# mLSTM and neighbourhood attention on one core: weights' low parts one item later, the first scores ahead of the last transposes, the closing norm's steps one item later on two engines

## The chip, the cores and the metric

The kernel runs on one core of a Trainium2 chip. The metric is the device time of one execution in microseconds (us): the median of three runs, beside which one more execution was profiled. A core has one instruction queue for each of its engines: TensorE (PE in the rows; PEld is its weight load), VectorE (DVE), ScalarE (ACT), GpSimd (POOL) and SyncE (SP, which here only issues DMAs). The queues run side by side and meet at semaphores: an instruction waits until a semaphore has reached a number, and raises one when it is done.

## What is computed

Two stacks of two layers follow one another on 256 tokens of width 1024. The change lies in the even mixer of the second stack, in two of its parts.

```python
def even_mixer(hx, hc, ...):              # hx: 256 latent tokens, hc: 256 context tokens
    naq, nak, nav, mlqk, mlv, mlo, mlg = split(h @ w_in)
    na_x = neighbourhood_attention(...)   # 8 heads of 64, latent queries: window + all context keys
    h_xf, h_xb = mlstm_chunked(...)       # 4 heads of 128, forward and backward, chunks of 128
    ml_x = _mlstm_output(h_xf + _rev(h_xb), mlo_x, ml_norm_g)
    y_x = concatenate([na_x, ml_x]) @ w_out
    na_c = dense_attention(...)           # context queries, context keys
    ...                                   # y_c likewise

def _mlstm_output(h, o_pre, g):           # the gate, then the closing norm over each head
    h = sigmoid(o_pre) * h
    mu = mean(h); var = mean(square(h - mu))
    return (h - mu) * rsqrt(var + EPS) * g
```

## The kernel before

All is float32; 512 tokens (256 context, 256 latent) lie in four tiles of 128. Products with large weights are split: of a weight tile RAW the high part WHI is a cast (ACT, `high`, L1516), the low part WLO = RAW - WHI a subtraction (DVE, `rest`, L2170), and TensorE adds three products of such halves. A unit is 1 MB of weights; `split(n)` makes TensorE wait for its low part, and SP loads a unit once the work on the unit that had its slot is done.

Each engine's program is written out by hand, so the order below is the order of the code. There are no pools and no scheduler.

**The mLSTM stage** has 16 items n, head h = n // 4 and query tile t = n % 4. For each, DVE makes the exponents' arguments (`args`, L2696 to L2701), ACT the exponentials (L1948, L1949), TensorE the scores (`score`), DVE weighs and normalises them (`weigh`, L2712 to L2723, result PR), TensorE transposes them (`turn(n)`, L1161), ACT copies the transposed tile out (`copy_turned`, L1927), and TensorE multiplies it with the values (`values(n)`). TensorE does `turn(n)` and then `values(n - 1)`. Between `score(n + 1)` and `turn(n)` it does six parts of the attention's input projections (`na_part`), which fill its time; ACT takes each finished tile of these out (`na_take`, L1934 and L1937). Six weight units, EVEN0 + 10 to EVEN0 + 15, are split in this stage, in the items ML_UNITS_AT = (1, 4, 6, 9, 12, 14): `high` is ACT's last work of such an item, `rest` DVE's. The first four of them are for `na_part`, the last two for the output projection. Once a head is complete, DVE multiplies it by the output gate (`gate(h)`, L2728, which waits for the head's last values).

**The attention stage** has 16 pairs p of heads (`EVEN_PAIRS`): eight with 256 keys, then eight with 512 keys and a bias. For pair p DVE finds two row maxima (`top(p)`, L2765, L2766), ACT makes the exponentials (`weights(p)`, L1986), DVE normalises them (`norm(p)`, L2773, L2775), TensorE transposes (`turn(p)`, L1245), ACT copies (L1996), TensorE multiplies with the values, ACT casts the high part of the result (`place_high`, L2002) and DVE subtracts for the low part (`place`, L2781). Orders by pair: TensorE `scores(p + 2), turn(p), values(p - 1)`; DVE `top(p + 1), norm(p), place(p - 2)`; ACT `weights(p + 1)`, copies of p, `place_high(p - 1)`. PR and PRE are two pairs of buffers, taken in turn.

**The closing norm** of the mLSTM (`head_norm`) is spread over the attention's pairs: after its own work each engine calls it with n = 2p - 2 and 2p - 1. For the four heads there is a mean product on TensorE (at n in MEAN_AT = 0, 3, 6, 9), a centring on DVE (L2747), a square on ACT (L1966); one variance product at n = 13; logarithm and exponential at 14 and 15 (ACT); then a product that spreads the inverse root (SPREAD_AT = 16, 19, 22, 25; weight operand HSTD), a scaling on DVE (L2751), a cast on ACT (L1976) and a subtraction on DVE (L2756). Every product of the norm goes to PSUM bank 7 and waits until DVE or ACT has read the one before.

After the last pair, the output projection waits for all 16 `place` and the four subtractions of the norm.

## Time and profile before

| | us |
|---|---|
| median of three runs | 2146.18 (2145.66 to 2146.91) |
| the profiled execution | 2143.44 |
| its span, first to last instruction | 2141.6 |
| PE busy in the span | 2097.8 |
| DVE busy in the span | 1525.0 |
| ACT busy in the span | 1060.0 |
| mLSTM stage in the span | about 1171 to 1281.5 |
| attention stage in the span | about 1281.5 to 1353.6 |

A row of the timeline gives the start of an instruction, or of several alike that follow one another, counted from the span's start, its time, the engine, the line, what is written and read, the count, and in brackets how long the engine was idle just before and who ended that. Durations of matmuls are modelled, and each overlaps the next; the distance between two starts says how long one occupies the engine. On DVE and ACT too a following instruction can start some 0.1 us before the row of the last one ends.

### The profile page before, as it was taken

To read this page: it belongs to the slowest core of one execution; us is meant where nothing else is said; L and a number is where in the kernel's file an instruction comes from. 1 tells how busy PE (TensorE), PEld (TensorE's weight loads), DVE (VectorE), ACT (ScalarE), POOL (GpSimd) and SP (SyncE) were. 2 spreads that over 40 slices of the span, in tenths; PEclk is the share of its full clock that TensorE was granted. 3 is DMA by queue.
4 is the path that set the end of the run, shared out by engine and by line. 5 is a ranking of instruction groups with operands and counts; after the bars stand their busy time and mean duration, and the time that the engine had idled before them with its cause. 6 is when DMAs were issued, how large, how long until landed. Compare 5 with 4: busy or idle time off the path is not lost.

```text
span 2141.6 us, 35228 instructions
## 1 busy us (share of the span) xinstructions
PE 2097.8 (98%) x14796; PEld 1922.4 (90%) x14796; DVE 1525.0 (71%) x2351; ACT 1060.0 (49%) x1578; POOL 156.1 (7%) x195
## 2 busy tenths in 40 slices
PE   9999999999999999999999998999999999999997
PEld 8999989999999998999997774898888888589997
DVE  7878888878988798998852666456555335857774
ACT  6443656443644465644462446345444334746663
POOL 1200102200210100210100000000000001000000
PEclk9999999999999999999999999999999999999999
DMA  7665526667566543777431120113222222123552
GB/s 286 231 238 203 209 99 249 243 228 273 193 241 230 206 177 118 282 269 264 149 111 66 60 68 38 49 58 132 99 99 99 99 79 95 43 79 122 190 182 99
DMA packets 48334, 334.93 MB, mean 156 GB/s; under 512 B 5612, under 2 KB 6716, under 8 KB 8880
## 3 DMA queue, kind: packets, MB, share of 16 engines
q1 hardware_dynamic: 38384, 267.47, 35.3%
q0 software_dynamic: 9792, 65.21, 8.1%
q8 instruction: 117, 1.92, 0.4%
q14 instruction: 41, 0.34, 0.0%
HBM read 331.61 MB, written 1.05 MB: 155 GB/s over the span
## 4 chain that ended last, share of the span: by engine, by line
PE 90%; DVE 5%; ACT 2%; issue 1%; DMA 0%; POOL 0%; DVEq 0%; ACTq 0%; POOLq 0%
PE PS L475 88%; PE PS L1245 1%; DVE WLO L2170 1%; ACT WHI L1516 1%; DVE STAT L2765 0%; DMA RAW<-in_up_a 0%; DVE TM L2712 0%; DVE AC L2613 0%; PE PS L1161 0%; DVE ACC L2410 0%; DVE TM L2696 0%; DVE PT L2454 0%; ACT X L1548 0%; DVE XB L2255 0%; DVE X L2597 0%
## 5 line engine op out<-in xcount | busy, mean ns | idle before, releaser
L2170 DVE TENSOR_TENSOR WLO<-RAW,WHI 128x2048 fp32r<-128x2048 f32 (+1 forms) x251 | 573.2, 2288 | 212.3 <-ACT WHI L1516 209.7
L475 PE MATMUL PS<-XB,WHI 128*128 128x256 f32 (+1 forms) x3136 | 703.6, 320 | 7.9 <-DVE WLO L2170 4.4
L1516 ACT CAST WHI<-RAW 128x2048 fp32r<-128x2048 f32 (+1 forms) x247 | 467.2, 1894 | 271.0 <-DMA RAW<-in_dn_c 75.4
L475 PEld LDWEIGHTS PS<-XB,WHI 128*128 128x128 f32 x3136 | 523.4, 191 | 52.9 <-issue 5.1
L475 PE MATMUL PS<-XHI,WHI 128*128 128x272 f32 (+1 forms) x1760 | 498.5, 290 | 0.1
L475 PE MATMUL PS<-XB,WLO 128*128 128x256 f32 (+1 forms) x1568 | 498.3, 318 | 0.0
L475 PE MATMUL PS<-XHI,WLO 128*128 128x272 f32 (+1 forms) x1760 | 489.4, 287 | 0.0
L475 PE MATMUL PS<-XLO,WHI 128*128 128x272 f32 (+1 forms) x1760 | 481.2, 287 | 0.0
L475 PEld LDWEIGHTS PS<-XHI,WHI 128*128 128x128 f32 x1760 | 328.4, 188 | 1.7 <-issue 0.7
L475 PEld LDWEIGHTS PS<-XHI,WLO 128*128 128x128 f32 x1760 | 325.7, 188 | 0.2
L475 PEld LDWEIGHTS PS<-XLO,WHI 128*128 128x128 f32 x1760 | 322.2, 188 | 1.4 <-DVE XLO L2216 0.8
L475 PEld LDWEIGHTS PS<-XB,WLO 128*128 128x128 f32 x1568 | 299.6, 191 | 20.1
L475 PE MATMUL PS<-GHI,WHI 128*128 128x272 f32 (+1 forms) x704 | 200.3, 286 | 0.0
L475 PE MATMUL PS<-GHI,WLO 128*128 128x272 f32 (+1 forms) x704 | 199.7, 285 | 0.0
L2613 DVE SCALAR_TENSOR_TENSOR AC<-CB,FCW,AC 128x512 f32<-128x512 f32 (+1 forms) x176 | 97.1, 614 | 133.7 <-ACT AC L1835 105.1
L475 PE MATMUL PS<-GLO,WHI 128*128 128x272 f32 (+1 forms) x672 | 191.9, 286 | 0.0
L475 PEld LDWEIGHTS PS<-GHI,WLO 128*128 128x128 f32 x704 | 132.5, 188 | 0.0
L475 PEld LDWEIGHTS PS<-GHI,WHI 128*128 128x128 f32 x704 | 132.4, 188 | 0.0
L2199 DVE CUSTOM_DVE_ANT_0 PROD<-AW,SCB,ADAB 128x1024 f32<-128x1024 f32 x96 | 131.4, 1368 | 0.0
L1623 ACT ACTIVATE SG<-PS 128x272 f32<-128x272 f32 (+1 forms) x88 | 34.5, 393 | 195.2 <-PE PS L475 194.8
L2199 DVE CUSTOM_DVE_ANT_0 AW<-AW,SCB,ADAB 128x1024 f32<-128x1024 f32 x96 | 127.1, 1324 | 0.0
L475 PEld LDWEIGHTS PS<-GLO,WHI 128*128 128x128 f32 x672 | 126.4, 188 | 0.0
(372 smaller groups left out, 2464.9 us busy)
## 6 DMA issues: line engine op xcount, KB each, us to landing
AW<-in_ada POOLq DMA_DIRECT2D x48, 1024.0 KB, 7.2
RAW<-in_up_c SPq DMA_DIRECT2D x44, 1024.0 KB, 4.9
RAW<-in_up_a SPq DMA_DIRECT2D x42, 1024.0 KB, 5.2
RAW<-in_up_b SPq DMA_DIRECT2D x42, 1024.0 KB, 5.0
RAW<-in_mix SPq DMA_DIRECT2D x30, 1024.0 KB, 4.9
RAW<-in_dn_a SPq DMA_DIRECT2D x22, 1024.0 KB, 4.9
RAW<-in_dn_b SPq DMA_DIRECT2D x22, 1024.0 KB, 4.9
RAW<-in_dn_c SPq DMA_DIRECT2D x22, 1024.0 KB, 4.9
```

The costliest lines, as they stand in the source:

```text
L475: return pe.matmul(o, w, x, start=first, stop=last)
L1245: last = pe.transpose(PS[:, 4 + e, j * P:(j + 1) * P], q[:, j * P:(j + 1) * P], IDN[:, :])
L1516: act.copy(WHI1[:, s, 0:w], RAW[:, s, 0:w]).then_inc(w1_high, 1)
L1623: act.activation(SG[r, f % 2, tk], PS[r, 2 * (f % 3), tk], ACT.Silu).then_inc(silu1_done, 1)
L2170: v.tensor_tensor(WLO1[:, s, 0:w], RAW[:, s, 0:w], WHI1[:, s, 0:w].bitcast(F32), ALU.subtract)\
L2199: v.tensor_tensor_reduce(PROD[:, :] if g == 0 else w, w, SCB[:, g, :], 1.0, ADAB[:, t:t + 1], ALU.mult, ALU.add, MODF[:, t, g:g + 1]).then ...
L2613: return v.scalar_tensor_tensor(o, i, vec(a, t), o, ALU.mult, ALU.add)
```

## The change

Nothing that is computed changes, and no arithmetic is added or removed. What moves:

- **Low parts.** In the mLSTM stage DVE's `rest` of a unit goes from the end of its item to the end of the next, and ACT's `high` goes ahead of `copy_turned` and `na_take` of the same item.
- **First scores.** TensorE does the first pair's scores ahead of `turn(15)` of the mLSTM; DVE's last gate goes behind the first pair's `top(0)`. The buffer sets PR and PRE change places, so that the first pair writes PRE while the mLSTM still holds PR; ACT's wait for the mLSTM's end goes from pair 0 to pair 1.
- **Closing norm.** DVE's three steps and ACT's square and cast come one n later. TensorE's products and the logarithm and exponential stay.
- **Last values.** The last pair's values go to bank 7, so that they wait for `place(13)` and the norm's last scaling, no longer for `place(14)`.

```diff
-        PRE_SETS = [PR, [place("G", f"PRE{n}", n * L2, [L2]) for n in range(2)]]
+        PRE_SETS = [[place("G", f"PRE{n}", n * L2, [L2]) for n in range(2)], PR]
...
+            if b < len(EVEN_PAIRS):
+                return PS[:, 6 + (b == len(EVEN_PAIRS) - 1), 0:P]
...
+            def first_scores():
+
+                pe.wait_ge(ml_bcopied, MLH)
+                pe.wait_ge(na_taken, 8)
+                for e, (a, b) in enumerate(EVEN_PAIRS[0]["qk"]):
+                    mm(pe, PS[:, 2 + e, 0:EVEN_PAIRS[0]["keys"]], a, b, True, True).then_inc(at_scores, 1)
...
                     na_part(NA_PARTS * n, NA_PARTS)
+                    if n + 1 == ML_ITEMS:
+                        first_scores()
                     turn(n)
...
-                    if base == 0 and b >= 1:
+                    if base == 0 and b == len(EVEN_PAIRS) - 1:
+                        pe.wait_ge(at_out, b - 1)
+                        pe.wait_ge(head_step, HEAD_Y[3])
+                    elif base == 0 and b >= 1:
                         pe.wait_ge(at_out, b)
...
@@ ACT, mlstm
+                    if n in ML_UNITS_AT:
+                        high(EVEN0 + 10 + ML_UNITS_AT.index(n))
                     if n >= 1:
                         copy_turned(n - 1)
...
-                    if n in ML_UNITS_AT:
-                        high(EVEN0 + 10 + ML_UNITS_AT.index(n))
                 copy_turned(ML_ITEMS - 1)
@@ ACT, head_norm
-                if n - 2 in MEAN_AT:
+                if n - 3 in MEAN_AT:
...
-                if n - 2 in SPREAD_AT:
+                if n - 3 in SPREAD_AT:
@@ DVE, mlstm
-                    if n in ML_UNITS_AT:
-                        rest(EVEN0 + 10 + ML_UNITS_AT.index(n))
-                gate(MLH - 1)
+                    if n - 1 in ML_UNITS_AT:
+                        rest(EVEN0 + 10 + ML_UNITS_AT.index(n - 1))
+                return lambda: gate(MLH - 1)
@@ DVE, head_norm
-                if n - 1 in MEAN_AT:
+                if n - 2 in MEAN_AT:
...
-                if n - 1 in SPREAD_AT:
+                if n - 2 in SPREAD_AT:
...
-                if n - 3 in SPREAD_AT:
+                if n - 4 in SPREAD_AT:
@@ DVE, attend
                 top(0)
+                behind_first()
                 for p in range(len(pairs)):
```

DVE at the seam of the two stages, before: WLO is the low part of unit EVEN0 + 15, TM and PR0 or PR1 belong to items 14 and 15, and G at L2728 is the last gate.

```order
L2723 SCALAR_TENSOR_TENSOR PR0_137<-TM0_141,STAT_115,PR0_137 128x384
L2170 TENSOR_TENSOR WLO1_77<-RAW_76,WHI1_78 128x2048
L2712 ISA TM1_142,STAT_115<-TM1_142,PS 128x512
...
L2723 SCALAR_TENSOR_TENSOR PR1_138<-TM1_142,STAT_115,PR1_138 128x512
L2728 TENSOR_TENSOR G_151<-G_151,PS 128x512
L2765 TENSOR_REDUCE STAT_115<-PS 128x1
```

The same place in the changed kernel, whose lines are numbered some 15 higher (L2738 is the old L2723, L2185 the old L2170, L2743 the gate, L2780 the maximum).

```order
L2738 SCALAR_TENSOR_TENSOR PR0_137<-TM0_141,STAT_115,PR0_137 128x384
L2727 ISA TM1_142,STAT_115<-TM1_142,PS 128x512
...
L2738 SCALAR_TENSOR_TENSOR PR1_138<-TM1_142,STAT_115,PR1_138 128x512
L2185 TENSOR_TENSOR WLO1_77<-RAW_76,WHI1_78 128x2048
L2780 TENSOR_REDUCE STAT_115<-PS 128x1
L2781 TENSOR_SCALAR STAT_115<-STAT_115 128x1
L2780 TENSOR_REDUCE STAT_115<-PS 128x1
L2781 TENSOR_SCALAR STAT_115<-STAT_115 128x1
L2743 TENSOR_TENSOR G_151<-G_151,PS 128x512
L2780 TENSOR_REDUCE STAT_115<-PS 128x1
```

The low part now stands behind item 15's weighing, and the gate behind the first pair's two maxima.

TensorE at the same seam, before: the last product of `na_part`, `turn(15)`, the values of items 14 and 15, then the scores of pairs 0, 1 and 2 (two rows of 256 for each pair) and pair 0's transposes.

```order
L475 MATMUL PS<-WHI1_78,XB_112 128x256
L1161 MATMUL PS<-IDN_113,PR1_138 128x128 x4
L475 MATMUL PS<-PTT0_139,VM_144 128x128 x4
L475 MATMUL PS<-PTT1_140,VM_144 128x128 x4
L475 MATMUL PS<-G_151 128x256 x6
L1245 MATMUL PS<-IDN_113,PR0_137 128x128 x2
```

And in the changed kernel:

```order
L477 MATMUL PS<-WHI1_78,XB_112 128x256
L477 MATMUL PS<-G_151 128x256 x2
L1170 MATMUL PS<-IDN_113,PR1_138 128x128 x4
L477 MATMUL PS<-PTT0_139,VM_144 128x128 x4
L477 MATMUL PS<-PTT1_140,VM_144 128x128 x4
L477 MATMUL PS<-G_151 128x256 x4
L1256 MATMUL PS<-IDN_113,PRE0_163 128x128 x2
```

Two of the six score products stand ahead of `turn(15)`; the first pair's buffer is PRE.

DVE in the attention stage at pairs 12 to 14, before: L2775 is the last of `norm(12)`, L2781 `place(10)`, L2756 and L2751 steps of the norm, L2765 and L2766 `top(14)`.

```order
L2775 TENSOR_SCALAR PR1_138<-PR1_138,STAT_115 128x512
L2781 TENSOR_TENSOR XB_112<-PS,XB_112 128x128
L2756 TENSOR_TENSOR XB_112<-G_151,XB_112 128x2x256
L2751 SCALAR_TENSOR_TENSOR G_151<-G_151,MLG_180,PS 128x512
L2765 TENSOR_REDUCE STAT_115<-PS 128x1
```

And in the changed kernel, where L2771 is the old L2756:

```order
L2790 TENSOR_SCALAR PRE1_164<-PRE1_164,STAT_115 128x512
L2796 TENSOR_TENSOR XB_112<-PS,XB_112 128x128
L2771 TENSOR_TENSOR XB_112<-G_151,XB_112 128x2x256
L2780 TENSOR_REDUCE STAT_115<-PS 128x1
...
L2796 TENSOR_TENSOR XB_112<-PS,XB_112 128x128
L2766 SCALAR_TENSOR_TENSOR G_151<-G_151,MLG_180,PS 128x512
L2780 TENSOR_REDUCE STAT_115<-PS 128x1
```

The scaling that stood in the same pair as the product it reads now stands one pair behind it.

## Rows read from the trace of the kernel before

**Rows 1.** The page, first part: busy time, share of the span, instructions.

```profile
PE 2097.8 (98%) x14796; PEld 1922.4 (90%) x14796; DVE 1525.0 (71%) x2351; ACT 1060.0 (49%) x1578; POOL 156.1 (7%) x195
```

**Rows 2.** Waits of PE, 1150 to 1400 us: total, times, longest in us.

```profile
PE PS L1161 <- DVE PR L2723: 5.6, 5, 2.0
PE PS L1245 <- DVE PR L2775: 5.3, 3, 2.7
PE PS L1245 <- DVE PRE L2775: 3.6, 4, 1.6
...
PE PS L475 <- DVE XB L2781: 1.5, 2, 0.8
```

**Rows 3.** Busy us (instructions) of PE, PEld, DVE, ACT, POOL; PEclk is granted clock.

```profile
1178.00:1181.40 3.40, 3.29 (x11) 1.35 (x9) 3.08 (x15) 1.01 (x3) 0.00 (x0) 1.00 0.00 0
1181.43:1184.84 3.41, 3.41 (x9) 2.37 (x8) 0.36 (x2) 0.65 (x2) 0.00 (x0) 0.50 0.02 5
1341.80:1345.20 3.40, 0.77 (x2) 0.00 (x0) 2.72 (x8) 1.84 (x5) 0.00 (x0) 1.00 0.43 116
1345.27:1348.68 3.41, 3.38 (x22) 3.06 (x24) 2.50 (x8) 1.36 (x4) 0.00 (x0) 0.50 0.48 197
```

**Rows 4.** Timeline: the chain to `turn(7)`, on ACT, DVE and PE.

```profile
1218.24 1.90 ACT L1516 CAST WHI<-RAW 128x2048 fp32r<-128x2048 f32 x1
1220.04 1.34 ACT L1948 ACTIVATE TM<-TM,STAT 128x512 f32<-128x512 f32 x2
...
1220.17 2.29 DVE L2170 TENSOR_TENSOR WLO<-RAW,WHI 128x2048 fp32r<-128x2048 f32 x1 [3.06 <-ACT WHI L1516]
...
1223.20 0.68 DVE L2712 CUSTOM_DVE_ANT_0 TM<-TM,PS 128x512 f32<-128x512 f32 x1
...
1225.65 0.75 DVE L2723 SCALAR_TENSOR_TENSOR PR<-TM,STAT,PR 128x512 f32<-128x512 f32 x1
...
1226.46 0.66 PE L1161 MATMUL PS<-IDN,PR 128*128 128x128 f32 x4 [1.96 <-DVE PR L2723]
```

**Rows 5.** Timeline: the third gate on DVE, and `turn(13)` on PE.

```profile
1260.25 0.69 DVE L2728 TENSOR_TENSOR G<-G,PS 128x512 f32<-128x512 f32 x1 [3.66 <-PE PS L475]
...
1266.47 0.44 PE L1161 MATMUL PS<-IDN,PR 128*128 128x128 f32 x2 [1.09 <-DVE PR L2723]
```

**Rows 6.** Timeline: first four maxima (first; reciprocal behind them) on DVE, third scores on PE.

```profile
1282.15 0.42 DVE L2765 TENSOR_REDUCE STAT<-PS 128x1 f32<-128x256 f32 x1
...
1284.24 0.15 DVE L2773 RECIPROCAL STAT<-STAT 128x1 f32<-128x1 f32 x1
...
1284.04 0.70 PE L475 MATMUL PS<-G 64*128 64x256 f32 x4 [1.49 <-ACT PR L1986]
```

**Rows 7.** Waits of DVE, 1280 to 1354 us: total, times, longest in us.

```profile
DVE G L2751 <- PE PS L475: 6.3, 2, 3.9
DVE XB L2756 <- ACT XB L1976: 5.0, 3, 2.4
DVE G L2747 <- PE PS L475: 4.1, 2, 2.2
```

**Rows 8.** Timeline: pairs 13 and 14 on PE, and the norm's subtraction on DVE.

```profile
1339.24 1.25 PE L1245 MATMUL PS<-IDN,PRE 128*128 128x128 f32 x8 [0.89 <-DVE PRE L2775]
1340.42 1.09 PE L475 MATMUL PS<-PTT,VN 128*64 128x128 f32 x16
...
1345.30 1.97 PE L1245 MATMUL PS<-IDN,PR 128*128 128x128 f32 x8 [2.73 <-DVE PR L2775]
1347.19 1.80 PE L475 MATMUL PS<-PTE,VN 128*64 128x128 f32 x16
...
1342.38 0.69 DVE L2756 TENSOR_TENSOR XB<-G,XB 128x512 fp32r<-128x512 f32 x1 [2.40 <-ACT XB L1976]
```

**Rows 9.** Timeline: the cast of a result and a square on ACT.

```profile
1307.09 0.27 ACT L2002 CAST XB<-PS 128x128 fp32r<-128x128 f32 x1 [0.17 <-PE PS L475]
1307.25 0.63 ACT L1966 ACTIVATE OSQ<-G 128x512 f32<-128x512 f32 x1
```

More of the change, by code:

```diff
@@ L220, in build @@
         VV = place("G", "VV", 10 * L2, [4, D])
-        PRE_SETS = [PR, [place("G", f"PRE{n}", n * L2, [L2]) for n in range(2)]]
-        PTE_SETS = [PTT, [place("G", f"PTE{n}", (2 + n) * L2, [4, P]) for n in range(2)]]
+        PRE_SETS = [[place("G", f"PRE{n}", n * L2, [L2]) for n in range(2)], PR]
+        PTE_SETS = [[place("G", f"PTE{n}", (2 + n) * L2, [4, P]) for n in range(2)], PTT]
         PRO_SETS = [[place("G", f"PRO{m}{n}", (18 - 10 * m + n) * L2, [L2]) for n in range(2)] for m in range(2)]
@@ L269, in values_of @@
         def values_of(b):
-            return PS[:, 6, 0:P] if b < len(EVEN_PAIRS) else PS[:, 6 + b % 2, 0:P]
+            if b < len(EVEN_PAIRS):
+                return PS[:, 6 + (b == len(EVEN_PAIRS) - 1), 0:P]
+            return PS[:, 6 + b % 2, 0:P]
         def na_pair(i, t):
@@ L1260, in values @@
                     last.then_inc(at_pv, 1)
-                scores(0)
+                if base:
+                    scores(0)
                 scores(1)
@@ L1956, in mlstm @@
                             na_take(i)
[L1957 to L1958 removed]
                 copy_turned(ML_ITEMS - 1)
             def head_norm(n):
[L1963 to L1964 removed]
+                if n - 3 in MEAN_AT:
+                    h = MEAN_AT.index(n - 3)
                     act.wait_ge(head_step, HEAD_CENTRED[h])
@@ L1972, in head_norm @@
                     act.activation(HSTD[:, :], HSTD[:, :], ACT.Exp, scale=-0.5).then_inc(head_act, 1)
-                if n - 2 in SPREAD_AT:
-                    h = SPREAD_AT.index(n - 2)
+                if n - 3 in SPREAD_AT:
+                    h = SPREAD_AT.index(n - 3)
                     act.wait_ge(head_step, HEAD_Y[h])
@@ L1980, in weights @@
                     w, c = pairs[p]["keys"], 48 * (p % 2)
+                    if base == 0 and p == 1:
+                        act.wait_ge(ml_turned, ML_ITEMS)
+                        act.wait_ge(ml_pv, ML_ITEMS)
                     for e in range(2):
@@ L2752, in head_norm @@
                                            ALU.mult, ALU.mult).then_inc(head_step, 1)
-                if n - 3 in SPREAD_AT:
-                    h = SPREAD_AT.index(n - 3)
+                if n - 4 in SPREAD_AT:
+                    h = SPREAD_AT.index(n - 4)
                     v.wait_ge(head_act, HEAD_STD + h + 1)
@@ L2757, in head_norm, with attend @@
                                     ALU.subtract).then_inc(head_step, 1)
-            def attend(pairs, base, probs, banks, between):
+            def attend(pairs, base, probs, banks, between, behind_first=lambda: None):
                 def top(p):
@@ L2918, in _ @@
             even_inputs()
-            mlstm()
-            attend(EVEN_PAIRS, 0, PRE_SETS, (2, 3, 0, 1), lambda n: head_norm(n - HEAD_SHIFT))
+            last_gate = mlstm()
+            attend(EVEN_PAIRS, 0, PRE_SETS, (2, 3, 0, 1), lambda n: head_norm(n - HEAD_SHIFT), last_gate)
             even_output()
```

8 lines of the change are left out of this document (2 added, 6 removed).

## The prediction, made before the changed kernel was run

> **What bounds the kernel now.** I read the busy times first. TensorE is busy for 2097.8 of 2141.6 us [rows 1], so the kernel ends when TensorE has done its work, and no more than the 43.8 us in which it idles can be gained by an order. The waits of TensorE over the two stages that the change touches show where some of this lies [rows 2]: 5.6 us in five waits before the mLSTM's transposes, and 8.9 us in seven waits before the attention's transposes (5.3 in three for PR, 3.6 in four for PRE), all ended by DVE; 1.5 us in two waits at the end for the low part of a result; and one wait of 1.49 us ahead of the third pair's scores [rows 6]. That is 17.5 us. Nothing else in these stages is idle on TensorE, and behind them its work is the same as before. So the question is how many of these waits go, and what is late next. The third thing to see is the clock: for 3.4 us from 1345.27 on it stands at 0.50, the lower level of 1.2 GHz [rows 3].
>
> **Low parts (mLSTM stage).** The five waits are for items 2, 7, 10, 13 and 15, each the one behind an item with a unit. Item 7 shows how one arises [rows 4]. ACT starts the unit's cast at 1218.24 and only 1.80 us later, at 1220.04, item 7's exponentials. DVE stands in front of the subtraction until the cast is there (3.06 us idle), subtracts from 1220.17 on for 2.29, makes the arguments of item 8, and starts to weigh item 7 at 1223.20; it is done at 1226.40 (1225.65 + 0.75), and TensorE, which waited 1.96 us, starts at 1226.46. TensorE was free at 1224.50.
>
> In the changed order the cast has been made earlier in ACT's queue, while ACT waited for TensorE's tile; the exponentials start where the cast stood, 1.8 us earlier, and end at about 1219.7 (1.34 and a short one behind). DVE has no subtraction in front and can weigh at once: 1219.7 plus its 3.2 us (1223.20 to 1226.40) is 1222.9, 1.6 us before TensorE is free. The wait of 1.96 goes whole. For item 13 [rows 5] DVE was held by the gate until 1260.25; then came 0.6 for the gate, 2.2 for the subtraction and the rest. Without the 2.2 the weighing ends 2.2 earlier, against a wait of 1.09, so 1.1 us is to spare. The other three waits are 2.6 us together (5.6 less 1.96 and 1.09), each under the 2.2 us of one subtraction that leaves the queue ahead of it, and go too.
>
> The work is not gone: the subtraction now stands behind the weighing of the item after. What it delays there is the arguments of the item after next and with them `turn(n + 2)`. Before, these had 2.2 us more behind a late start; counted from TensorE's own earlier schedule, item 14 is the tight one, since TensorE comes to it 1.1 us earlier than before while DVE, held by the gate, is no earlier; I leave 0.3 us there, and bound it by 0 and by the 1.1 us of [rows 5]. ACT's copies of transposed tiles now wait behind a cast of 1.90 [rows 4]. TensorE needs such a copy only after its next six parts, which take over 4 us (its free time at 1224.50 less the previous item's end), so the cast is hidden; if a unit's load came late, ACT would stand in front of it and this cover would be gone (below). Gain of this part: 5.6 - 0.3 = 5.3 us, between 4.3 and 5.6.
>
> **First scores and last gate (the seam).** Between the mLSTM's last values and pair 1's transposes TensorE now waits 1.49 [rows 6] and 0.43 (the 8.9 us of [rows 2] less the six waits below). DVE needs four maxima behind the gate, 1282.15 to 1284.24, 2.1 us, before its first reciprocal [rows 6]. In the changed order two of them stand ahead of the gate, in time in which DVE waited for the last values. Behind the last values: gate 0.6, two maxima 1.05, one normalisation 0.5, handover 0.1, so the first transposes can start 2.3 us after them; TensorE's own work till then is the scores of two pairs instead of three, 1.1 us. That leaves a wait of 1.2, and a second of 0.5 for pair 1, whose normalisation stands behind two more maxima (1.05). 1.7 against 1.92: a gain of 0.2 us, bounds -0.5 and 1.0. The two score products themselves cost the same in either place. The last subtraction of a unit (2.29 [rows 4]) now stands in front of `top(0)`; it starts when item 15 is weighed, as TensorE ends its projections or before, so it ends close to the first scores' end, and the values of items 14 and 15 (2 us) hide what is left.
>
> **Closing norm (attention stage).** Six waits (1.65, 1.65, 0.89, 0.61, 0.89, 2.73) make 8.4 of the 8.9 us [rows 2]. They lie at the transposes of pairs 2, 5, 10, 11, 13 and 14. In each case DVE has stood, in the pair before, in front of a step of the norm whose product TensorE issues in that same pair (L2747: 4.1 us in two waits, L2751: 6.3 in two), or whose cast ACT makes in that same pair (L2756: 5.0 in three) [rows 7]; the maxima and the normalisation queued behind it come late. Pair 14 is the worst [rows 8]: DVE waits 2.40 for a cast until 1342.38, and TensorE 2.73 until 1345.30. One n later, all four centrings and all four scalings stand a pair behind their products. The first four waits and the 2.73 lose their cause: 1.65 + 1.65 + 0.89 + 0.61 + 2.73. What is late next:
> - A subtraction still stands in the same pair as its cast for two heads, at pairs 12 and 15. At pair 12 it costs what it cost at pair 10 to 13 before, 0.6 to 0.9; I take 0.75 before `turn(13)`, where 0.89 stood.
> - Pair 14 on DVE carries a subtraction (0.69 [rows 8]) and a scaling of about the same between two normalisations, with no maxima left to make: about 2.1 us against the 2.0 or less of TensorE's transposes and values. I take 0.4 before `turn(14)` and 0.5 before `turn(15)`.
> - The variance product now waits for the last square, which comes behind the cast of pair 6: 0.17 of the cast, 0.63 of the square [rows 9] and 0.15 for two handovers, 0.95 us.
> - The end: the last values no longer wait for `place(14)` (0.78 of the 1.5 us [rows 2]). The output projection waits for the last cast, subtraction and two `place`, which start with the high part of pair 14: 0.2 + 0.6 + 0.6 + 0.2 + 0.3 + handovers, 2.05, against the last values' 1.0: 1.05 instead of 0.7.
>
> So 8.4 + 1.5 = 9.9 us of waits become 0.75 + 0.4 + 0.5 + 0.95 + 1.05 = 3.65. Gain 6.2 us. If the variance and the two last pairs cost nothing it is 8; if pairs 12 to 15 cost 2.73 once more, it is 4.
>
> **Clock.** The lower level from 1345.27 on follows a stretch in which TensorE was busy 0.77 of 3.40 us [rows 3]. In it the transposes took 1.97 and the values 1.80, against 1.25 and 1.09 for the same work one pair before [rows 8]: 1.43 us. The longest wait that I leave in the stage is 1.2 us, so I let this go: gain 1.4, bounds -1.4 and 1.4.
>
> The Trainium skill ("TensorE: Matmul & The Clock Gate", the section "Why this matters for your kernels") says to avoid throughput drops by leaving no long idle gaps between bursts of matmuls. By that rule alone every fall of the clock comes from a gap, and the 1.4 us go with the gap. Here the trace agrees in one place and not in the other, since from 1181.43 on the clock is at 0.50 too, behind a stretch in which TensorE was busy for 3.29 of 3.40 us, with transposes and products of four rows [rows 3]. So a fall without a gap is a rival below.
>
> **The sum.** 5.3 + 0.2 + 6.2 + 1.4 = 13.1 us. Against the profiled execution's 2143.44 that is 2130.3; against the median of 2146.18, which lies 2.7 higher for the same kernel, 2133.1. Loads keep their distance: units EVEN0 + 14 to 17 and the bias tables are released by TensorE's own progress and move with it.
>
> **The rivals.**
> 1. The clock falls once in the changed stages all the same (in its attention stage much is transposes and narrow products): nothing gained on it, 2134.5; twice, 2135.9. For it: 1181.43. Against: most of the stage has the same mix now and keeps the full clock. Chance 0.16.
> 2. The low parts only move the waits: weighing of item n + 2 comes as late as that of n + 1 did. Then 5.3 shrinks to about 0.5: 2138. For it: DVE's work per item is the same. Against: its waits for casts (3.06 in item 6 [rows 4]) were idle time, which goes. 0.08.
> 3. The norm's new places only move the waits (variance, pairs 12 to 15, end): 6.2 and 1.4 shrink to about 1: 2139.7. Against: the waits of [rows 7] have a cause by order, which is gone for five of six. 0.08.
> 4. Both shrink, gain under 4.3 us: 2142 to 2150. 0.05.
> 5. Slower. Bank 7 holds one product at a time, and TensorE's next mean or spread product waits for DVE's step, which now stands a pair later. If DVE came to it only after TensorE's values of that pair, TensorE would stand at three means, the variance, three spreads and the last values. Between the last normalisation and the next product TensorE has transposes and values, 1.2 us with 256 keys, and DVE a `place` and the step, 0.2 + 0.7: 0.3 to spare. The whole gain is lost, and 4.3 more, if each of the eight places costs over 2.2 us ((13.1 + 4.3) / 8); 1 us at each, 8 in all, would give 2141. Taken at 2.5 each: 2153. Chance 0.03.
>
> **How the numbers follow.** The forecast 2133 has 0.60. A measurement of this kernel can tell about 0.2% from no change, 4.3 us. Forecast and rivals 1 to 3 gain more than that: faster 0.92; rival 4 is within it, 0.05; rival 5 slower, 0.03. The range: all bounds at their best are 5.6 + 1.0 + 8 + 1.4 = 16, 2130; with half a us for the spread of medians 2129.5. At the other end rivals 1 to 3 are taken in: 2140.5.
>
> **What would show it.** In the changed trace: no wait of TensorE for DVE's PR in the mLSTM stage, or at items 13 and 14 alone; DVE's idle time in front of the low parts gone; a wait of about 1.2 us before pair 0's transposes; no waits of 1.65 at pairs 2 and 5; a new one of about 1 us at the variance product, ended by ACT's square; 0.4 to 0.8 before the transposes of pairs 13 to 15; about 1 us ahead of the output projection; and the full clock up to it but for the fall near 1181. I am wrong if TensorE's waits between 1170 and the projection stay over 9 us, or if ACT stands in front of a unit's cast for its load.

## The result, and the profile after

The changed kernel took 2129.23 us (median of four runs, 2127.28 to 2129.82), the kernel before in the same comparison 2146.55 (four runs, 2145.66 to 2149.22). The ratio is 0.9916, with a 95% interval of 0.9899 to 0.9933: 17 to 18 us less. Forecast were 2133.1 and a range from 2129.5 to 2140.5, so the sign was right and the time lies 0.3 us below the range. Over all its runs the changed kernel has a median of 2128.71 (8 runs), and the kernel before has 2145.77 over the 70 runs of the experiments below: 17.1 us, where the forecast's sum has 13.1. The profiled execution took 2129.82 us, its span is 2128.0; the forecast made against a profiled execution was 2130.3.

First part of the page of the changed kernel, in answer to [rows 1]: busy time, share, instructions.

```profile
PE 2095.9 (98%) x14796; PEld 1921.2 (90%) x14796; DVE 1525.3 (72%) x2351; ACT 1057.8 (50%) x1578; POOL 155.7 (7%) x195
```

The span is 13.6 us shorter and TensorE's busy time 1.9 us, so idle time is most of what went, but not all of it. The waits of PE from 1150 to 1400 us, in answer to [rows 2] (total, times, longest):

```profile
PE PS L1256 <- DVE PRE L2790: 1.5, 2, 1.2
PE PS L1256 <- DVE PR L2790: 1.4, 3, 0.6
PE PS L477 <- DVE XB L2796: 1.1, 1, 1.1
```

The five waits of the mLSTM stage are gone: there is no row for its transposes (L1170 now). Of 17.5 us of waits, the 1.49 before the third scores [rows 6] included, 4.0 are left. The timeline of PE has them one by one, in brackets:

```profile
1278.99 0.90 PE L1256 MATMUL PS<-IDN,PRE 128*128 128x128 f32 x4 [1.25 <-DVE PRE L2790]
1280.96 1.15 PE L1256 MATMUL PS<-IDN,PR 128*128 128x128 f32 x4 [0.43 <-DVE PR L2790]
...
1329.38 1.25 PE L1256 MATMUL PS<-IDN,PR 128*128 128x128 f32 x8 [0.61 <-DVE PR L2790]
1333.00 1.25 PE L1256 MATMUL PS<-IDN,PRE 128*128 128x128 f32 x8 [0.29 <-DVE PRE L2790]
1335.65 1.25 PE L1256 MATMUL PS<-IDN,PR 128*128 128x128 f32 x8 [0.38 <-DVE PR L2790]
1339.93 0.50 PE L477 MATMUL PS<-XB,WHI 128*128 128x256 f32 x2 [1.14 <-DVE XB L2796]
```

They are those of pairs 0, 1, 13, 14, 15 and of the output projection, for which the forecast left 1.2, 0.5, 0.75, 0.4, 0.5 and 1.05. A seventh doesn't show in brackets, since it lies within a group of products of one form. The timeline at the variance product:

```profile
1301.26 0.66 PE L477 MATMUL PS<-PTE,VN 128*64 128x128 f32 x8
1301.84 2.01 PE L477 MATMUL PS<-OSQ,ONES 128*32 128x512 f32 x8
...
1302.12 0.63 ACT L1980 ACTIVATE OSQ<-G 128x512 f32<-128x512 f32 x1
1302.81 0.14 PEld L477 LDWEIGHTS PS<-OSQ,ONES 128*32 128x32 f32 x2 [0.81 <-ACT OSQ L1980]
1303.78 0.70 PE L477 MATMUL PS<-G 64*128 64x512 f32 x2
```

Eight products begin at 1301.84, but the last of the four squares, which they read, is made from 1302.12 to 1302.75, and only then does the load of the last weights follow. From here to the next row are 1.94 us; in r7 below, where no square is awaited, the same group takes 1.00. So 0.95 us is wait, though it counts as busy.

The two stages as a whole, in windows from the first work of the mLSTM stage to the projection (busy us of PE, PEld, DVE, ACT, POOL; PEclk). The kernel before:

```profile
1171.11:1281.50 110.39, 104.66 (x579) 84.50 (x578) 70.55 (x249) 46.96 (x91) 0.00 (x0) 0.98 0.19 66
1281.50:1353.60 72.10, 60.10 (x409) 34.84 (x409) 48.05 (x157) 43.57 (x123) 2.68 (x5) 0.98 0.14 51
```

The changed kernel:

```profile
1172.20:1276.62 104.42, 104.31 (x582) 84.82 (x581) 71.52 (x253) 47.77 (x95) 0.00 (x0) 0.98 0.19 67
1276.62:1339.93 63.31, 59.18 (x405) 34.09 (x405) 47.14 (x153) 41.91 (x119) 2.65 (x5) 0.97 0.18 64
```

Both stages together fell from 182.49 to 167.73, 14.76 us. The idle time of PE (length less busy) fell from 17.73 to 4.24, 13.5 us; less the 0.95 hidden in the variance product that is 12.55 of waits. The other 2.2 us are busy time. Part of it is plain in the rows: four transposes take 0.90 in the rows above and [rows 8]'s eight 1.25 behind a wait, against 0.60 (r8, below) and 1.04 without one (the changed kernel's pairs 8 to 12). The single instructions show why. DVE normalises the two heads of a pair one after the other; here are the two of pair 13 in the kernel before:

```profile
1338.70 0.49 DVE L2775 TENSOR_SCALAR PRE<-PRE,STAT 128x512 f32<-128x512 f32 x1
...
1339.29 0.49 DVE L2775 TENSOR_SCALAR PRE<-PRE,STAT 128x512 f32<-128x512 f32 x1
```

TensorE starts the first head's four transposes at 1339.24, as DVE ends the first, and the second head's at 1339.84, as DVE ends the second (1339.29 + 0.49 is 1339.78). That is 0.21 us behind the fourth, where one transpose follows another at 0.11. So a row behind a wait holds a second, short wait inside it, which counts as busy; and after either start the second transpose comes at 0.17 instead of 0.11. Over the 984 products that both kernels have here, counted from start to start without the bracketed idle time, the transposes fell from 20.70 to 19.24 us, the variance product grew by 0.94 and the mean products by 0.84, behind the fall of the clock described next, and all others together fell by 1.6. The span is shorter by 13.6 only, since the changed kernel came to these stages 1.1 us later, behind a fall of its clock at 1165 us.

The clock did not do what was forecast. A "fall" is a stretch in which the granted clock is at 0.50. The one at 1345.27 behind pair 14's wait [rows 3] is gone, but the changed kernel has one in the same stage at 1281.39, behind the waits of pairs 0 and 1. Up to the last 25 us of the program either profile has three falls of 3.41 us, two of them in the windows above: before at 1072, 1181 and 1345, after at 1165, 1182 and 1281. So between these two profiles the clock gained nothing, and the 14.76 us are waits and busy time alone. The fall at 1281.39, and the stretch before it:

```profile
1278.00:1281.38 3.38, 1.93 (x10) 0.90 (x10) 3.14 (x15) 2.69 (x10) 0.03 (x1) 1.00 0.87 293
1281.39:1284.80 3.41, 3.39 (x13) 1.51 (x12) 2.08 (x9) 1.94 (x7) 0.00 (x0) 0.50 0.78 324
```

### The profile page after: what moved, and what is told of

Its sections match the earlier page's. It is cut to its first block, busy times and chain, and to the rows that moved or that the text cites. A ratio compares the mean times of both kernels' runs of the same rounds, so it can differ in the third digit from the quotient of the medians.

```text
span 2128.0 us, 35229 instructions
## 1 busy us (share of the span) xinstructions
PE 2095.9 (98%) x14796; PEld 1921.2 (90%) x14796; DVE 1525.3 (72%) x2351; ACT 1057.8 (50%) x1578; POOL 155.7 (7%) x195
## 3 DMA queue, kind: packets, MB, share of 16 engines
HBM read 331.61 MB, written 1.05 MB: 156 GB/s over the span
## 4 chain that ended last, share of the span: by engine, by line
PE 90%; DVE 4%; ACT 2%; DMA 2%; issue 1%; POOL 0%; SPq 0%; DVEq 0%; ACTq 0%; POOLq 0%
PE PS L477 89%; PE PS L1256 1%; DMA NG<-in_norm_g 1%; DVE WLO L2185 1%; DMA RAW<-in_up_a 0%; POOL SUM L580 0%; DMA RAW<-in_mix 0%; PE PS L1170 0%; ACT WHI L1530 0%; DVE AC L2628 0%; DVE ACC L2425 0%; DVE PT L2469 0%; ACT X L1562 0%; DVE STAT L2780 0%; DMA PL<-in_x 0%
## 5 line engine op out<-in xcount | busy, mean ns | idle before, releaser
L2185 DVE TENSOR_TENSOR WLO<-RAW,WHI 128x2048 fp32r<-128x2048 f32 (+1 forms) x251 | 573.4, 2289 | 198.8 <-ACT WHI L1530 195.4
```

The lines of the kernel that those rows point to most:

```text
L2185: v.tensor_tensor(WLO1[:, s, 0:w], RAW[:, s, 0:w], WHI1[:, s, 0:w].bitcast(F32), ALU.subtract)\
```

## Experiments

Three groups of kernels, each beside its own runs of the kernel before. Parts of the change come first, each alone, then the whole. A gain that stands behind a ratio is worked out from the ratio; the difference of the medians can be 1 to 2 us from it.

**r1: the kernel before, unchanged.** Was the base of the forecast right?

> The kernel before once more, unchanged. Question: the forecast from the profiled execution (2143.44 less 13.1 is 2130.3, measured 2129.8) held, the one from the median (2146.2 less 13.1 is 2133.1, measured 2129.2) did not. Theory A, the profiled execution of before was a lucky one: executions of one kernel scatter by 1 to 3 us with where TensorE's clock falls to half, each fall costing 1.4 to 1.7 us. Then this profile has another set of falls, or the same number at other places, its time lies between 2143 and 2149, and outside the falls its instructions lie within 0.3 us of the first profile's. Theory B, the offset of 2.7 us is a constant of the profiled execution: then this kernel's profiled time is again 2.7 us under its median. Ratio to before 1.000 within 0.0015 by either.

Measured: 2145.90 (12 runs), and 2144.98 over the 31 other runs of the kernel before beside it; ratio 1.0001 (0.9990 to 1.0012). Its profiled execution took 2150.11. A constant distance of 2.7 us between profiled and other executions is refuted: here the profiled one lies 4 us above. That is beyond theory A's own range of 2143 to 2149 too, since the scatter is wider than it had it. The windows around the attention stage's start tell why:

```profile
1283.60:1287.05 3.45, 2.03 (x12) 1.03 (x12) 3.21 (x15) 2.83 (x11) 0.10 (x1) 1.00 0.92 306
1287.09:1300.74 13.65, 12.10 (x44) 5.58 (x44) 7.53 (x30) 5.91 (x21) 1.60 (x3) 0.50 0.27 100
```

The clock stands at 0.50 for 13.65 us, and once more for 3.41 at 1307.57. Instruction by instruction this execution is 6.6 us behind the first one at its end, and 5.8 of it come in between 1240 and 1306 us. Over 70 runs of the kernel before, the mean granted clock and the time go together:

| granted clock | 0.991 | 0.992 | 0.993 | 0.994 | 0.995 | 0.996 |
|---|---|---|---|---|---|---|
| runs | 4 | 7 | 3 | 24 | 17 | 15 |
| median us | 2152.4 | 2149.6 | 2148.2 | 2146.6 | 2144.7 | 2144.0 |

The forecast's own profiled execution, at 0.996, is among the least disturbed: 15 of these 70 have that clock, and only 5 are faster than its 2143.44.

**r2: low parts alone.**

```diff
@@ ACT, mlstm
+                    if n in ML_UNITS_AT:
+                        high(EVEN0 + 10 + ML_UNITS_AT.index(n))
                     if n >= 1:
                         copy_turned(n - 1)
...
@@ DVE, mlstm
-                    if n in ML_UNITS_AT:
-                        rest(EVEN0 + 10 + ML_UNITS_AT.index(n))
+                    if n - 1 in ML_UNITS_AT:
+                        rest(EVEN0 + 10 + ML_UNITS_AT.index(n - 1))
```

> The kernel before with the first part of the change alone: ACT's cast of a unit ahead of its copies, DVE's subtraction one item later. Order theory: the five waits of 5.6 us before the mLSTM's transposes go, and the attention stage keeps its seven waits of 8.9 us: about 5.5 us faster, 2140.7, if no wait of DVE takes their place. Rival, the waits only move: under 1 us faster, and new waits ended by DVE before transposes of items 3, 6, 8, 11, 14.

Measured: 2140.26 (10 runs), ratio 0.9973 (0.9963 to 0.9983), 5.8 us less (3.6 to 7.9). No wait of PE is left in the mLSTM stage.

**r3: the closing norm's steps alone** (the five numbers in the two `head_norm` of the diff; last values and seam as before).

> The kernel before with the closing norm's steps alone one n later on DVE and ACT. Order theory: six waits of 8.4 us before the transposes of pairs 2, 5, 10, 11, 13, 14 become about 1.6 us at pairs 13 to 15, and the variance product waits 0.95; a removed wait gives back 0.2 us more, since the transposes behind it run as two separate pairs: 6 to 7 us faster, and 1.4 more if the clock does not fall near the end of the stage. 2138.5 to 2140. Rival, the product of the next head waits for the late step: under 3 us faster.

Measured: 2139.05 (6 runs), ratio 0.9965 (0.9953 to 0.9978), 7.5 us less (4.7 to 10.1). The waits before pairs 2, 5, 10, 11 and the 2.73 are gone; the last values, which here still wait for `place(14)`, have 1.90, and behind that wait the clock falls. Timeline, and windows, of this kernel:

```profile
1344.47 1.75 PE L475 MATMUL PS<-PTE,VN 128*64 128x128 f32 x16 [1.90 <-DVE XB L2781]
```

```profile
1341.30:1344.70 3.40, 1.50 (x23) 1.12 (x23) 0.89 (x2) 1.65 (x4) 0.00 (x0) 1.00 0.05 19
1344.75:1351.58 6.83, 6.15 (x38) 5.75 (x34) 3.51 (x3) 3.86 (x3) 0.15 (x2) 0.50 0.00 0
```

This is what the other bank for the last values is for: with the norm moved alone, the wait at `place(14)` grows from 0.78 to 1.90.

**r4: first scores and last gate alone** (`first_scores`, the gate behind `top(0)`, the exchanged buffers).

> The kernel before with the seam alone: first scores ahead of the last transposes, last gate behind the first maxima, buffer sets exchanged. Order theory: the waits of 1.49 and 0.43 become 1.2 and 0.5, and item 15's wait of 1.28 shrinks by the 0.6 of the scores made in it: 0.6 to 1.0 us faster, 2145.4. Rival, the seam carries part of the 4 us that the change gave beyond the forecast: 3 us faster or more.

Measured: 2145.46 (10 runs), ratio 0.9997 (0.9987 to 1.0007). A gain of 0.6 is as likely as none; the waits are those forecast, 1.24 before pair 0 and 0.43 before pair 1 in place of 1.49 and 0.43. The three parts alone add up to 5.8 + 7.5 + 0.6 = 13.9 us, and the whole gives 17.1. Two things forbid reading this as parts that help each other: by the intervals of the three ratios the sum is uncertain by some 4 us, and a fourth part, the other bank for the last values, is in none of the three. That part was never run alone; r3 shows what its absence costs, a wait of 1.90 us and a fall of 6.83 behind it, neither of which the whole has.

**r5: the changed kernel again.**

> The changed kernel once more, beside more runs of the kernel before. Theory (the median of three runs that the forecast started from lay some 1.2 us above the kernel's own, 2145.0 over 31 runs; the order's gain is 13.1 us by the forecast's terms, and some 1 us more since a transpose that follows a wait costs 0.2 us more than one that doesn't): 14 to 15.5 us less than the kernel before, 2129.5 to 2131, a ratio of 0.9928 to 0.9935; in the profile the falls of the clock stand elsewhere in part than in the first profile, while the waits of TensorE between 1150 and 1345 us are the same ones within 0.2 us each. Rival (the changed kernel loses less to the clock than the kernel before, on top of the order): 15.5 to 18 us less, a ratio of 0.9916 to 0.9927, and in nearly all of its runs a granted clock of 0.995 to 0.997, where the kernel before has 0.991 to 0.996.

Measured: 2128.28 (2126.84 to 2129.04, 4 runs) beside 2146.66 (9 runs), ratio 0.9912 (0.9897 to 0.9926). That is the rival's answer and even past its edge (18.4 us by the medians beside it, 17.5 against the 70 runs), and with it falls what was thought after r1, that the base was 1.2 us too high: over 70 runs it is 2145.77, 0.4 below the 2146.18 of the forecast. The waits of PE are the same to 0.02 us; the falls at 1182 and 1281.39 are not there. That gives the price of a fall, since nothing else differs. The same two stages, from the same first product to the projection:

```profile
1172.84:1337.39 164.55, 160.33 (x985) 117.31 (x984) 118.50 (x406) 89.62 (x214) 2.66 (x5) 1.00 0.19 67
```

They take 164.55 us without a fall and 167.73 with two: 1.6 us for each. All its runs have a granted clock of 0.996, and so have 7 of the 8 of the changed kernel.

**r6: all but the norm's steps.**

> The changed kernel with the closing norm's steps where they were before (low parts, seam and the last pair's bank changed). Theory (the parts add up): 0.6 of the seam and 5.8 of the low parts, as measured apart, so 6 to 7.5 us less than before, 2137.5 to 2139, a ratio near 0.997; in the profile six waits of TensorE before the attention's transposes are back, 8 to 9 us, the longest again 2.7 us before the transposes of pair 14. Rival (the parts help each other, for instance because the earlier seam gives the norm's steps room): over 8.5 us less, and the six waits together under 7 us.

Measured: 2140.66 (6 runs), ratio 0.9966 (0.9954 to 0.9979), 12.4 us more than r5 on the same chip. The six waits are back, 8.4 us with the longest 2.73, as the theory has it; the median is 1.7 us above its range. The norm's steps are worth 12.4 us on top of the rest and 7.5 alone (r3), where the last values' wait and the fall behind it eat part of them. Beside r5, idle time explains half: 10.8 us of waits of PE against 4.0 + 0.95, 5.9 us. The clock has a large share of the rest. This kernel's profile has three stretches at the lower level in the attention stage, 13.7 us together, r5's none. The last begins at 1342.08, in the last 0.7 us of pair 14's wait of 2.73:

```profile
1338.60:1342.04 3.44, 1.40 (x10) 0.39 (x4) 2.17 (x6) 1.50 (x4) 0.00 (x0) 1.00 0.29 71
1342.08:1348.90 6.82, 6.17 (x36) 5.19 (x38) 4.07 (x12) 3.70 (x9) 0.00 (x0) 0.50 0.30 123
```

**r7: the changed kernel with ACT's two steps where they were.** DVE's stay one later.

```diff
@@ ACT, head_norm
-                if n - 3 in MEAN_AT:
-                    h = MEAN_AT.index(n - 3)
+                if n - 2 in MEAN_AT:
+                    h = MEAN_AT.index(n - 2)
...
-                if n - 3 in SPREAD_AT:
-                    h = SPREAD_AT.index(n - 3)
+                if n - 2 in SPREAD_AT:
+                    h = SPREAD_AT.index(n - 2)
```

> The changed kernel with ACT's squares and casts of the closing norm where they stood before (two numbers behind the product), and DVE's steps one later as in the changed kernel. Then no square stands behind a later pair's weights and no subtraction waits in the same pair as its cast. Theory (the waits left in the attention stage come from ACT's own delay): the wait of about 0.95 us inside the variance product, those of 0.6, 0.3 and 0.4 us before the transposes of pairs 13 to 15 and some 0.3 of the 1.1 us ahead of the output projection go; 2.5 to 3.5 us less than the changed kernel. Rival (ACT now stands in front of DVE's centring, and the weights queued behind it come late): waits of TensorE for ACT's copies or weights at pairs 1 to 12, and a time that is the same as the changed kernel's or up to 3 us more.

Measured: 2123.90 (2123.07 to 2125.15, 4 runs), ratio to the kernel before 0.9892 (0.9878 to 0.9907): the fastest of all, with every run under every one of the changed kernel. Its waits of PE, 1150 to 1400:

```profile
PE PS L1256 <- DVE PRE L2790: 1.2, 1, 1.2
PE PS L477 <- DVE XB L2796: 0.7, 1, 0.7
PE PS L1256 <- DVE PR L2790: 0.4, 1, 0.4
```

The waits at pairs 13 to 15 are gone, the projection's is 0.7 instead of 1.1, and the variance product is whole:

```profile
1297.55 0.16 PEld L477 LDWEIGHTS PS<-OSQ,ONES 128*32 128x32 f32 x8 [0.17 <-issue]
1297.56 1.06 PE L477 MATMUL PS<-OSQ,ONES 128*32 128x512 f32 x8
```

Against r5, instruction by instruction, the attention stage is 3.4 us shorter, within the 2.5 to 3.5 of the theory; the 4.4 between the medians of four runs each may hold some of the 1.8 us by which its profiled execution is ahead before these stages, where both kernels are the same. So the step that should move was DVE's. ACT's two steps were not late before; moved along, they made a square and casts late.

**r8: the first wait of the attention stage filled, in the changed kernel.** `keep_busy(n, bank)` issues n products of 256 rows of a constant tile, ONES, into a PSUM bank.

```diff
+                    if base == 0 and p == 0:
+                        keep_busy(9, 4)
                     turn(p)
```

> The changed kernel with nine products of 256 rows that nobody reads ahead of the first pair's transposes, in the 1.25 us in which TensorE waits there; they go to a bank that those transposes overwrite. Nothing else is moved. Theory (the falls of the clock in the attention stage follow the idle time at its start): the fall that stood at 1281 us in the changed kernel's profile is gone, there is none between 1280 and 1310 us, and the time is 0 to 1.5 us less than the changed kernel's. Rival (falls there come with the kind of work, transposes and narrow products, and not with the idle time): a fall in that stretch as before, and the same time within 0.5 us, or up to 0.5 us more for the products.

Measured: 2128.42 (4 runs), ratio 0.9913 (0.9898 to 0.9928), the same as r5 by four runs each. It settles nothing on the falls: there is none in its stage, but neither is there in r5's. And its size was wrong. The timeline shows two instructions for each product and 0.43 us a product:

```profile
1277.29 4.15 PE L477 MATMUL PS<-ONES 128*128 128x256 f32 x18
1281.28 0.60 PE L1256 MATMUL PS<-IDN,PRE 128*128 128x128 f32 x4
```

Nine of them fill 3.9 us where 1.25 were free. This is not free of cost: instruction by instruction against r5, the products behind them come 2.7 us later, of which 1.0 is won back by pair 1, so that the stage is 1.6 us longer. The medians of four runs don't show it, which also says how little they can tell. The filled row does show, though, that four transposes take 0.60 once no wait stands before them, against 0.90.

**r9: the kernel before in its own order, its attention waits filled.** This is the test that r8 was not: no order changes, only the idle time.

```diff
+                        if base == 0 and e == 0:
+                            keep_busy({2: 3, 5: 3, 10: 2, 11: 1, 13: 2, 14: 6}.get(p, 0), 4)
                         pe.wait_ge(at_probs, n + 1)
...
+                    if base == 0 and p == 0:
+                        keep_busy(3, 4)
                     if p + 2 < len(pairs):
                         scores(p + 2)
```

> The kernel before in its own order, with products that nobody reads put into TensorE's waits of the attention stage: three ahead of the third scores (wait of 1.49 us), three before the transposes of pairs 2 and 5 (1.65 each), two at pairs 10 and 13 (0.89), one at pair 11 (0.61) and six at pair 14 (2.73). One such product took 0.43 us in r8_filled_seam, where nine of them overran the wait, so each wait is filled but for 0.0 to 0.4 us and none is overrun. They go to a bank that the transposes behind them overwrite. Theory (the falls of the clock between 1280 and 1355 us come behind idle time of TensorE; the kernel before loses 3 us or more to them, by 0 to 20 us at the lower level in its profiles, and the changed kernel next to nothing): at most one fall in that stretch, none behind pair 14's transposes, the granted clock of most runs at 0.996, and 2.5 to 4.5 us less than the kernel before, of which 1 to 1.5 us by transposes that no longer follow a wait. Rival (the falls come with the kind of work, or by chance, and the changed kernel has fewer only because it has less of what causes them elsewhere): falls as in the kernel before, behind pair 14's transposes for one, and 0 to 1.5 us less.

Measured: 2142.57 (11 runs) beside 2145.76 (18 runs), ratio 0.9983 (0.9974 to 0.9991), 3.2 us less by the medians. Of its eleven runs nine have 0.996 or 0.997, of the kernel before beside it four of eighteen. Its profile has no fall in the attention stage. Pair 14:

```profile
1344.80 2.86 PE L475 MATMUL PS<-ONES 128*128 128x256 f32 x12
1347.60 1.31 PE L1247 MATMUL PS<-IDN,PR 128*128 128x128 f32 x8
1348.84 1.09 PE L475 MATMUL PS<-PTE,VN 128*64 128x128 f32 x16
```

The transposes and values that took 1.97 and 1.80 [rows 8] take 1.31 and 1.09. The theory holds in its main point: work that computes nothing, put into waits, makes this kernel faster (1.9 to 5.6 us by the interval), and the clock of the stage is full. A part of it does not: no 1 to 1.5 us come from quicker transposes. A filled wait still ends as DVE ends the first head, so the rows stay long (0.90 and 1.31), and up to pair 14 the filled kernel falls 0.4 us behind the kernel before; at pair 14 it wins 1.4. The two stages take 181.26 us in its profile against 182.49, so most of the 3.2 us between the medians must lie in falls that other executions of the kernel before have and this profile of it hadn't. The profiled execution itself, 2145.30, is the slowest of the eleven, for reasons ahead of the stages: it is 2.2 us behind the kernel before's when they begin, 1.1 of it from a fall of 6.83 at 1071.

The places of the falls say the same. All seven profiles of kernels that keep the wait of 2.73 before pair 14 have a fall that begins there, from 0.65 us before the wait's end to 0.46 behind it, and no other profile has one within pair 14's work, but for r3's at the last values' wait of 1.90. The mean clock between 1277 and 1356 us in the profiles, by kernel:

| attention's waits | kernels | clock |
|---|---|---|
| as before | before, r1, r2, r4, r6, r10, r11 | 0.98, 0.87, 0.87, 0.96, 0.91, 0.96, 0.98 |
| moved, but 1.90 at the last values | r3 | 0.96 |
| as changed | after, r5, r7, r8 | 0.98, 1.00, 1.00, 1.00 |
| before, filled | r9 | 1.00 |

The row of r9 and that of the kernel before:

```profile
1277.00:1356.00 79.00, 74.64 (x503) 46.95 (x502) 51.73 (x168) 46.43 (x127) 2.81 (x7) 1.00 0.16 59
```

```profile
1277.00:1356.00 79.00, 65.71 (x454) 40.13 (x454) 50.76 (x165) 47.14 (x126) 2.83 (x7) 0.98 0.17 58
```

**r10 and r11: the two halves of the low parts' move.** r10 has only ACT's cast early (the first part of r2's diff), r11 only DVE's subtraction late (the second).

> Of the low parts' move only ACT's half: the unit's cast ahead of the copies of the turned tiles, and DVE's subtraction where it was, ahead of the next item's weighing. Theory (each wait has two causes in a row on two engines; the cast's 1.9 us and the subtraction's 2.2): DVE's idle time before the subtraction goes, but the subtraction still stands ahead of the weighing; the wait before item 7's transposes falls from 1.96 by up to 1.8, that of item 13, which the gate sets, stays at 1.1; 1 to 2 us of the 5.6 us of waits are left, and the time is 3 to 4.5 us less than before. Rival (the cast alone was the cause): no wait left in the stage but item 13's, and as much gain as both halves together, 5 us or more.

> Of the low parts' move only DVE's half: the subtraction one item later, ACT's cast where it was, 1.8 us ahead of the next item's exponentials. Theory (the same two causes): the exponentials of item 7 still start at the same distance behind the cast; DVE weighs at once when they are there, 3.2 us, which ends within 0.3 us of TensorE's need; 0 to 1 us of the 5.6 us of waits are left, and the time is 4 to 5.5 us less than before. Rival (DVE now stands in front of the exponentials instead of the cast, for as long): over 3 us of waits left, all ended by the same weighing, and under 3 us of gain.

Measured: r10 2138.59 (5 runs), ratio 0.9965 (0.9951 to 0.9978), with one wait of 1.1 us left in the stage, item 13's; r11 2138.96 (6 runs), ratio 0.9970 (0.9958 to 0.9982), with 0.9 us in two. Either half alone removes 4.5 us or more of the 5.6. For r10 that is the rival's answer, not the theory's. Both times lie lower than the waits alone give (7.2 and 6.8 us under the median beside them), but with 5 and 6 runs they are uncertain by some 3 us, so the waits decide here and not the times. The timeline of r10 at item 7:

```profile
1213.46 1.91 ACT L1516 CAST WHI<-RAW 128x2048 fp32r<-128x2048 f32 x1 [3.11 <-DMA RAW<-in_even]
...
1215.41 2.29 DVE L2170 TENSOR_TENSOR WLO<-RAW,WHI 128x2048 fp32r<-128x2048 f32 x1 [0.48 <-ACT WHI L1516]
...
1216.05 1.34 ACT L1948 ACTIVATE TM<-TM,STAT 128x512 f32<-128x512 f32 x2
...
1220.88 0.75 DVE L2723 SCALAR_TENSOR_TENSOR PR<-TM,STAT,PR 128x512 f32<-128x512 f32 x1
```

DVE stood 3.06 us in front of this subtraction before [rows 4] and stands 0.48 now, so the subtraction lies in what was idle time and ends at 1217.7, not in the way of the weighing, which is done at 1221.6 while TensorE comes to it at 1222.16. The 1.8 us by which the cast moved and the 2.3 us of the subtraction's place were not two causes that add up; each alone was more than the wait. Only item 13, where the gate holds DVE, needs the subtraction out of the way, as the forecast has it for that item.

## Why the prediction was near, and what it missed

**Low parts (5.3 forecast).** The five waits of 5.6 us are all gone, and r2 measures 5.8 with the 0.3 for item 14 not needed. For item 7 in the changed kernel:

```profile
1216.28 1.91 ACT L1530 CAST WHI<-RAW 128x2048 fp32r<-128x2048 f32 x1 [3.43 <-DMA RAW<-in_even]
...
1218.83 1.34 ACT L1962 ACTIVATE TM<-TM,STAT 128x512 f32<-128x512 f32 x2
...
1222.86 0.75 DVE L2738 SCALAR_TENSOR_TENSOR PR<-TM,STAT,PR 128x512 f32<-128x512 f32 x1
1223.53 2.28 DVE L2185 TENSOR_TENSOR WLO<-RAW,WHI 128x2048 fp32r<-128x2048 f32 x1
...
1224.66 0.60 PE L1170 MATMUL PS<-IDN,PR 128*128 128x128 f32 x4
```

The order is the forecast one. The weighing ends at 1223.6, 1.05 us before TensorE comes to it at 1224.66; forecast were 1.6 us to spare. The thing that was named as a sign of being wrong did happen: ACT stands 3.43 us in front of this cast until its load has come. It cost nothing here. The forecast had not worked out when the load comes, so this part was right with less to spare than it said.

**Seam (0.2).** 1.25 and 0.43 against 1.2 and 0.5; r4 agrees, within its error.

**Closing norm (6.2).** The terms left were 0.75, 0.4, 0.5, 0.95 and 1.05, 3.65 in all; measured 0.61, 0.29, 0.38, 0.95 and 1.14, 3.37. DVE stands 4.12 us before the cast of pair 12 and 2.40 before the last, where the forecast has it:

```profile
1326.47 0.69 DVE L2771 TENSOR_TENSOR XB<-G,XB 128x512 fp32r<-128x512 f32 x1 [4.12 <-ACT XB L1990]
...
1338.79 0.69 DVE L2771 TENSOR_TENSOR XB<-G,XB 128x512 fp32r<-128x512 f32 x1 [2.40 <-ACT XB L1990]
```

The forecast also named ACT's square and cast as what is late next, and r7 confirms it by taking them back. All waits that go, together: 11.7 forecast, 12.55 measured. The rival of the bank held too long didn't happen: TensorE waits at none of the norm's products but the variance's.

**Busy time (no term): the first step that failed, and the larger.** The prediction opens with the claim that no more than TensorE's idle time can be gained by an order, and its sum holds waits and the clock alone; it gives no reason for putting the work behind the waits at the same length. The runs show 2.2 us there, over half of the 4.0 that the sum lacks. A transpose row behind a wait costs 0.2 to 0.3 us more than one behind work; [rows 8] had 1.25 for pair 13, and a pair that waits for nothing, beside it, would have shown it. The waits before transposes went from twelve to five, and TensorE's busy time in the stages fell by 1.26 us though it now holds the variance's 0.95: 2.2 us. The transposes' own 1.5 hold 0.7 of pair 14's fall, so some 1.0 is theirs by r5, whose stages have no fall (18.99 us, against 20.70 less 0.72). The rest is spread over the other products.

**Clock (1.4, bounds -1.4 and 1.4): the second step that failed.** With 14.8 us of waits and busy time shown by the rows of the stages, 2.3 of the 17.1 are left for the clock, 0.9 more than the term and more than its best bound. This is a difference, not a row of its own. It was sized from one execution's only fall in the stage and bounded by one fall more or less. That execution was among the kernel's least disturbed: other profiles with the same waits have 3.4 to 20.5 us at the lower level between 1277 and 1356. At equal granted clock (0.996) the medians are 2143.98 (15 runs) and 2128.43 (7 runs), 15.6 us, near those 14.8; the remaining 1.5 come since most runs of the kernel before lie below 0.996 and those of the changed kernel don't. So the bound should have been taken from the scatter of runs. The mechanism of the term was right, as r9 shows; its size and its bound were not.

**The sum.** 0.85 us of waits, 2.2 of busy time and 0.9 of the clock make the 4.0 us between 13.1 and 17.1. The measured time lies only 0.3 us below the range, so either of the two steps, put right, would have taken it in. Two small slips of reckoning change nothing: 5.6 less 1.1 is 4.5 and not 4.3, and 6.2 less 2.73 is 3.5 and not 4.

Rival 1, a fall in the changed stages all the same, happened in the first profile and not in the second. It cost 1.6 us, where 1.4 was said. That the profiled 2129.8 and the forecast 2130.3 meet is luck, with misses of both signs (2.2 of busy time and 0.85 of waits gained; the clock's 1.4 and 1.1 ahead of the stages lost).

**The rule weighed.** The falls in the attention stage go the way of the rule of the Trainium skill ("TensorE: Matmul & The Clock Gate", the section "Why this matters for your kernels"): leave no long idle gap between bursts of matmuls. The trace agrees that idle time brings them, and r9 shows cause and effect, but with waits of 0.6 to 2.7 us each, none of them long. The rule doesn't cover the fall that starts between 1165 and 1184 us, of which there is at least one in all thirteen profiles: in the kernel before it stands behind dense work [rows 3], in the changed kernel's profile the one at 1165 stands behind 3.40 us in which TensorE was busy throughout. Its cause stays open.

## What to carry to other kernels

Where a step on engine B waits for a product of engine A made in the same round, move B's step one round later, but ask for each engine apart whether its step is late; one that already stands behind its input has only to lose (r7). Price a wait at its length, the slower start of the work behind it and a share of the clock falls that it brings; that share is read from the scatter of many runs, not from one profile. Before two causes are added, ask whether one alone is longer than the wait (r10, r11).

## What the runs showed of the hardware

- The 70 executions of the kernel before spread over 2142.9 to 2152.6 us, and their granted clock over 0.996 to 0.991: some 1.7 us for each thousandth, by the medians of the table. The falls in the middle of the program last 3.41, 6.83 or 13.65 us.
- A fall of 3.41 us cost 1.4 us behind pair 14's wait, where TensorE had full work, 1.6 us each in the two stages (r5 against the first profile of the same kernel), and 0.6 us at 1072, by aligning two executions.
- Nine products of 0.43 us that nobody reads, 3.9 us in a wait of 1.25, made the stage 1.6 us longer, which the medians of four runs did not show (r8: ratio 0.9913, r5: 0.9912); twenty of them in the kernel before, put into its waits, gained 3.2 us (r9).
- Eight transposes take 1.04 us behind work and 1.25 behind a wait of 0.3 to 0.9 us, at the full clock, since TensorE then waits for the second head's numbers inside the row.
